# Pads in the memory map: where the two operand tiles of the large products start, modulo 512 bytes

## What is computed

```
x = first_block(x, mem, ...)    # 2 layers: swiglu, gated delta rule or latent attention, swiglu
x = second_block(x, ...)        # swiglu, hybrid mixer (SSM + block attention), swiglu, layer norms
return third_block(x, ...)      # 2 layers: swiglu, gating unit or pooling mixer, swiglu

def swiglu(x, w_gu, w_down):    # the form of all ten, inner width 2816
    gate, up = jnp.split(x @ w_gu, 2, axis=-1)
    return (jax.nn.silu(gate) * up) @ w_down
```

## The kernel before, in words

| tile | start mod 512 | used as | moving minus stationary, mod 512 |
|---|---|---|---|
| `input_hi` | 160 | moving, 256 columns | 32 |
| `input_hi` | 160 | stationary, 512 and 256 columns | 480 |
| `hidden_hi` | 256 (288 in the first `ffn`) | stationary, 512 | 384 (352) |
| `y_hi` | 256 | moving, 256 | 128 |
| `mem_hi` | 288 | moving, 256 / stationary, 256 | 160 / 352 |
| `latent_hi`, `latent_q_hi` | 256 | moving, 256 | 128 |
| `attended_hi` | 320 | moving, 256 | 192 |
| `sgu_out_hi` | 0 | stationary, 512 | 128 |
| `pooled_hi` | 128 | stationary, 512 / moving, 256 | 0 / 0 |

## Time and profile before

### The profile page before, as it was taken

The page is one execution under the profiler, slowest core; times in us unless marked ns, Lnnn a source line. Parts: engine busy times, 40 slices in busy tenths (PEclk is TensorE's granted clock), DMA queues, the critical chain, the costliest instruction groups (busy, mean ns, idle before and its releaser), DMA issues. The chain is left out here.

```text
span 2913.7 us, 47309 instructions
## 1 busy us (share of the span) xinstructions
PE 2827.3 (97%) x20443; PEld 2624.9 (90%) x20443; DVE 1796.8 (62%) x2467; ACT 1492.0 (51%) x2011; POOL 26.5 (1%) x41
## 2 busy tenths in 40 slices
PE   8999999999998999999999999999999999999999
PEld 7998978999986999999998988989999899998898
DVE  5557756566566656555678655566556655656655
ACT  6447435455455545443575634454454544544643
POOL 1000000000000000000001000000000000000000
PEclk9999999999999999999999999999999999999999
DMA  6555115555552556555452455555555555554553
GB/s 231 184 175 162 52 44 186 187 166 181 188 161 87 179 188 203 190 188 171 138 182 92 145 169 194 188 173 188 188 177 176 170 188 187 182 189 150 196 189 129
DMA packets 370110, 489.12 MB, mean 168 GB/s; under 512 B 15424, under 2 KB 329186, under 8 KB 369776
## 3 DMA queue, kind: packets, MB, share of 16 engines
q1 hardware_dynamic: 368944, 485.90, 51.9%
q0 software_dynamic: 640, 0.20, 0.0%
q10 hardware_dynamic: 320, 0.01, 0.0%
HBM read 485.02 MB, written 1.05 MB: 167 GB/s over the span
## 5 line engine op out<-in xcount | busy, mean ns | idle before, releaser
L873 PE MATMUL work<-input_hi,weights_hi 128*128 128x256 f32 x3424 | 959.5, 280 | 1.8 <-DVE weights_lo L241 1.7
L876 PE MATMUL work<-input_hi,weights_lo 128*128 128x256 f32 x3424 | 956.2, 279 | 0.0
L875 PE MATMUL work<-input_lo,weights_hi 128*128 128x256 f32 x3424 | 955.9, 279 | 0.0
L231 DVE TENSOR_TENSOR weights_lo<-weights_raw,weights_hi 128x2048 fp32r<-128x2048 f32 (+2 forms) x282 | 629.5, 2235 | 320.1 <-ACT weights_hi L211 319.6
L873 PEld LDWEIGHTS work<-input_hi,weights_hi 128*128 128x128 f32 x3424 | 643.6, 188 | 6.8 <-DVE weights_lo L241 2.1
L875 PEld LDWEIGHTS work<-input_lo,weights_hi 128*128 128x128 f32 x3424 | 643.5, 188 | 4.4
L876 PEld LDWEIGHTS work<-input_hi,weights_lo 128*128 128x128 f32 x3424 | 643.5, 188 | 0.0
L215 ACT ACTIVATE weights_hi<-weights_raw,params 128x512 fp32r<-128x512 f32 (+2 forms) x736 | 462.0, 701 | 329.7 <-DMA weights_raw<-in_ffn_w_in 164.0
L211 ACT ACTIVATE weights_hi<-weights_raw 128x2048 fp32r<-128x2048 f32 (+2 forms) x282 | 524.0, 1864 | 169.3 <-DMA weights_raw<-in_ffn_w_up 101.1
L241 DVE SCALAR_TENSOR_TENSOR weights_lo<-weights_raw,params,weights_hi 128x512 fp32r<-128x512 f32 (+2 forms) x736 | 492.6, 733 | 168.6 <-ACT weights_hi L215 168.5
L334 PE MATMUL acc<-weights_hi,hidden_hi 128*128 128x512 f32 x880 | 349.6, 397 | 7.5 <-DVE hidden_lo L1049 5.7
(11 more groups left out here) (565 smaller groups left out, 3462.3 us busy)
## 6 DMA issues: line engine op xcount, KB each, us to landing
weights_raw<-in_ffn_w_gu SPq DMA_DIRECT2D x176, 512.0 KB, 4.7
weights_raw<-in_ffn_w_in SPq DMA_DIRECT2D x176, 512.0 KB, 4.7
weights_raw<-in_ffn_w_down SPq DMA_DIRECT2D x66, 1024.0 KB, 4.9
weights_raw<-in_w_in SPq DMA_DIRECT2D x44, 1024.0 KB, 5.3
weights_raw<-in_ffn_w_out SPq DMA_DIRECT2D x44, 1024.0 KB, 4.9
weights_raw<-in_a_w_in SPq DMA_DIRECT2D x29, 1024.0 KB, 5.5
weights_raw<-in_ffn_w_gate SPq DMA_DIRECT2D x44, 512.0 KB, 3.9
weights_raw<-in_ffn_w_up SPq DMA_DIRECT2D x44, 512.0 KB, 5.0
```

The source lines that it names most:

```text
L231: last = self.nc.vector.tensor_tensor(self.wl[:, n % SLOTS, 0:kc * cols], raw, self.wh[:, n % SLOTS, 0:kc * cols].bitcast(F32), ALU.subtract)
L873: nc.tensor.matmul(o, wh[:, k, ms], K.hi[:, c, :], start=(c == 0 and m == 0), stop=False, skip_group_check=True)
L875: nc.tensor.matmul(o, wh[:, k, ms], K.lo[:, c, :], start=False, stop=False, skip_group_check=True)
L876: last = nc.tensor.matmul(o, wl[:, k, ms], K.hi[:, c, :], start=False, stop=(c == DC - 1), skip_group_check=True)
```

## The change

A function `home(stack, remainder)` is added. It looks at where the next tile would start and, where that is not `remainder` modulo 512, allocates an unused tile "gap" that fills the difference. It is called ahead of the activation tiles of the large products. `MOVING` is 320 and `STATIONARY` is 448; the weights stay at 128. With the activation moving, the distance is 320 - 128 = 192. With `hidden`, `sgu_out` and `pooled` stationary and the weights moving it is 128 - 448 = -320, which is 192 modulo 512. No instruction of any engine is added, removed or moved.

```diff
+UNIT = 512
+MOVING, STATIONARY = 320, 448
@@ class Core
         self.h = self.sb("h", [P, DC, T])
+        self.home(ctx, MOVING)
         self.hi = self.sb("input_hi", [P, DC, T], F32R)
         self.lo = self.sb("input_lo", [P, DC, T], F32R)
...
         self.head_rows = self.sb("ssm_rows", [P, 3, SH])
+        self.home(ctx, MOVING)
...
+    def home(self, stack, remainder):
+        base = -(-self.nc.sbuf_base // 32) * 32
+        gap = (remainder - base) % UNIT
+        if gap:
+            stack.enter_context(self.fresh("gap", [P, gap // 4], F32))
@@ def ffn
         gr, sg, hid = tile("gate_r"), tile("silu"), tile("hidden")
+        K.home(e, STATIONARY)
         hh, hl = tile("hidden_hi", F32R), tile("hidden_lo", F32R)
@@ memory keys, latent keys, latent mixer, attention, SSM: each ahead of its hi tile
+        K.home(e, MOVING)        # mem_hi, latent_hi, latent_q_hi, attended_hi, y_hi
@@ gating mixer, pooling mixer: each ahead of its hi tile
+        K.home(e, STATIONARY)    # sgu_out_hi, pooled_hi
```

More of the change, by code:

```diff
@@ L2141, in __init__ @@
         self.lat, self.squares, self.roots = sb("latent", [P, 2, T]), sb("latent_squares", [P, 2, T]), sb("latent_roots", [P, 2, T])
+        K.home(e, MOVING)
         self.hi, self.lo = sb("latent_hi", [P, 2, T], F32R), sb("latent_lo", [P, 2, T], F32R)
```

## The result

The changed kernel takes 2902.7 us (median of 4 runs, 2899.6 to 2906.8) against 2917.9 us. The ratio is 0.9941 with a 95% interval of 0.9926 to 0.9957: 15 us less, where 55 were forecast and the range ended at 2888.

A forecast was written before the change was run, and what follows sets the result against it. TensorE's matmul stream, PE 97% busy, was taken as the bound. The span 2913.7 - 47 (256 columns) - 8 (512 columns) = 2858.7, plus 4.8 = 2863.5, about 2863 us; range 2849 to 2888.

The forecast's parts named there:

- What bounds the kernel: Whole kernel: TensorE's stream of matmuls sets the time, PE busy 97% of 2913.7 us, DVE 62%, ACT 51%.
- Step 1: Products of 256 columns, activation moving, distance 32 to 192: 13248 matmuls, 3.4 ns less each, 45.0 us gained.
- Step 2: 384 `y` matmuls from 118.6 to 113.4 ns: 2.0 us gained; `mem` and the two latent tiles 0.8 us.
- Step 3: 2832 matmuls of 512 columns, `hidden` and `sgu_out` stationary, distance to 192: 8 us gained, between 0 and 15.6.
- Step 4: `input` stationary, 480 to 320, 432 matmuls of 512 columns and 720 of 256: 0, between 6 us gained and lost.
- Step 5: `pooled` moving, 48 matmuls, can gain 0.3 us; `pooled` stationary, 96 matmuls, can lose 0.7 us: together 0.
- Step 6: Other tiles move by multiples of 32 bytes: element-wise operations unaffected, small float32 products under 1 us; both at 0.
- Step 7: Faster `ffn` steps need weights at 194 GB/s, not 188; no engine or queue near its limit, so nothing given back.
- Two ports, no contact: Rival: moving stream and weight load don't meet, `attended`'s 113.3 ns has another cause; no change, 2918 us; chance 0.08.
- the gain is handed to another engine: Rival: ACT or DVE late with `weights_lo`, half the gain goes into PE's waits: about 2891 us; chance 0.05.
- slower: Rival: the good distance belongs to `accumulate`'s alternation of eight outputs, 192 is bad for the `ffn` forms: 2963 us; chance 0.05.
- The sign of being wrong: Trace after, line 873: durations staying at 280 would mean the distance isn't the cause; 276 was forecast.

The follow-up runs named there:

- the probe: Whole computation left out: turns of 24 matmuls of 512 columns, then 96 of 256 with the moving tile at 192; the 256-column steps took 113.3 or 117.8 ns.
- the moving pads alone: Against the changed kernel, only the moving tiles are put at 320; hidden, sgu_out and pooled stay at 256, 0 and 128 as before: 2880.7 us, ratio 0.9872.

## Why the prediction was wrong

Point by point. The steps of after are means over all steps in the trace, waits left out.

- **What bounds the kernel.** Right. PE is 97% busy in both the earlier trace rows, the busy times of DVE and ACT are within 3 us of before, and the sum of the steps gives the time (below).
- **Step 1, activation moving: wrong, and it is the error.** It put 113.3 to all 13248 matmuls because one stretch of 186 had it. 192 allows 113.3 and 117.8, and the changed kernel has one half of each. Means: from 116.8 to 115.7 ns on the `ffn` lines, from 116.9 to 115.7 on the others: 10272 x 1.06 + 3192 x 1.15 = 14.6 us in place of 45.0. (The count was misread too: in the earlier trace rows the 960 of line 274 are `input` alone, `mem` and `pooled` have groups of their own, and 72 more write to `acc`. There are 13464, not 13248; that is 0.7 us.) The 186 matmuls were one draw, not 186: the rhythm was picked once, at the stream's start. I also read the 3 ns between a median of 276 and means of 279 as support from 3424 matmuls. It was the same stretch compared with lines at another distance.
- **Step 2, `y`.** 118.6 to 117.8 in place of 113.4: 0.3 us, not 2.0. It has the long rhythm, and has it in all seven traces of kernels with `y_hi` at 320 or 64. `mem` and the two latent tiles gained some 0.7 us together, about what was said. `attended`, counted as unchanged, lost 0.8 us, a draw of this trace and not the change's doing.
- **Step 3, 512 columns.** The middle was 8 us gained, the ends 0 and 16. It was a loss: 232.6 to 233.1, 2832 x 0.5 = 1.4 us. The end that said "as disturbed as the other distances" was the right one. Worse, the step was priced by itself. What the place of `hidden` costs stands in the stream behind it: with `hidden` left where it was, 36 us are gained instead of 15.
- **Step 4, `input` stationary at 320.** Taken as 0, measured as a gain: 512 columns from 233.1 to 229.5, 256 columns from 118.3 to 117.7, together 432 x 3.6 + 720 x 0.7 = 2.1 us. The range of 6 us held it.
- **Step 5, `pooled`.** Near what was said: 0.4 us lost.
- **Step 6, other tiles.** Right: line 1005, the old 994, has 611, 634 and 638 ns as minimum, median and maximum.
- **Step 7, gain not given back.** Right in what it says of engines and queues; the gain is lost inside PE's own stream.
- **The sum again**: -14.6 - 0.3 - 0.7 + 0.8 + 1.4 - 2.1 + 0.4 = -15.1 us. Measured: 14.3 us less at equal clock, 15.3 between the medians.
- **The rivals.** "Two ports, no contact" forecast no change and is refuted in that: tiles alone move and the time changes by 15 and 36 us. The Trainium skill ("TensorE: Matmul & The Clock Gate", Part 2) says that loading the next weights doesn't steal read bandwidth from the running matmul. What I drew from it, that the distance can't matter, isn't what these runs show: in a probe with nothing but matmuls a step goes from 113.3 to 120.0 ns by the distance of the two operands. Whether reads meet was not measured. The time lies nearest to "the gain is handed to another engine" (2891), but that rival's sign isn't there: the wait for `weights_lo` is 1.8 us against 1.7. The rival "slower" had a part of the truth, that 192 needn't be good for the `ffn` streams; its reason, the alternation of eight outputs, isn't needed, since the probes write one output and have both rhythms. The rival that was missing is the real one: the step depends on the distance and on the start.
- **What would have warned me.** `pooled` in the trace of before, after a wait, needs seven to nine matmuls of 512 columns before it runs at 226.7 ns, and the stream at distance 32 goes through 117, 120, 113 and 116 ns again and again where its distance modulo 512 doesn't change at all. Both speak for a step that depends on the one before.
- **The sign of being wrong.** "If durations on line 873 stay at 280, the distance isn't the cause" was wrong as well. They stayed at 280, and the distance is a cause: with the moving pads alone the same line has 277.

What stays open is the mechanism inside. The runs show that the step changes with the place of the moving and the stationary operand against each other modulo 256 bytes and, at some distances, with the way a stream begins. A contact of the two reads in SBUF fits that, but no run looks into it. Nor do they tell the reads of the moving tile from those of the weight load: every matmul here has one, and its reads weren't measured by themselves.

## What to carry to other kernels

Where back-to-back matmuls bound a kernel, look at the steps from start to start, not at durations, and lay out the two operands' starts on purpose; here 256-column float32r matmuls cost 113.3 to 120.0 ns and 512-column ones 226.7 to 234.4 by that and by how the stream began. Don't judge a layout by one stream: run it from several beginnings and with the streams that come before it, and change the place of one tile at a time, since a tile can harm a stream that never reads it. A pattern that looks like many equal samples may be one draw.

## What the runs showed of the hardware that was not expected

- float32r matmuls with the distance at 192 modulo 256 hold one of two steady rhythms, 113.3 or 117.8 ns for 256 columns, over a whole stream of 96 to 192. At a distance of 32 there are two as well, 116.7 and 117.8.
- The distance counts modulo 256: `far0b` and `far256b`, `far64b` and `far320b` agree, and the changed kernel with all pads 256 bytes off takes 2901.4 us against 2902.7.
- For 512 columns the best distance is 0 (226.7 ns, from every beginning) and for 256 columns 0 is the worst together with 96 (120.0).
- Behind 512-column matmuls at distance 0 an inserted matmul of 64 columns, which costs some 0.1 us with the settling behind it, saves 0.4 us in the 96 that follow (turns of 16.47 against 16.75 us in the probe). Widths of 16, 32, 128 and 160 columns don't.
- The span of the changed kernel moved by 7.2 us between executions whose mean granted clock was 0.994 and 0.997.
